# Convolution steps of a DeltaNet layer, moved one by one between VectorE's other work

## The reference

```python
h = jnp.einsum('btd,dc->btc', x, w_in)
qa, ka, va, za, ba, aa, qb, kb, vb, zb = jnp.split(h, offsets, axis=-1)
ya = _deltanet_group(qa, ka, va, za, ba, aa, conv_w, a_log, dt_bias, norm_w)
yb = _swa_group(qb, kb, vb, zb, sinks)
y = jnp.einsum('btc,cd->btd', jnp.concatenate([ya, yb], axis=-1), w_out)
return _layernorm(DEEPNORM_ALPHA * x + y, ln_g, ln_b)
```

```python
v_new = u_c - jnp.einsum('bhcd,bhde->bhce', w_c, s)
o = jnp.einsum('bhcd,bhde->bhce', q_c, s) + jnp.einsum('bhcs,bhse->bhce', qk_c, v_new)
s = s * gt[..., None, None] + jnp.einsum('bhcd,bhce->bhde', k_c, v_new)
```

## Time and profile before

| | |
|---|---|
| runs (3), median | 1091.87 us |
| lowest to highest | 1090.0 to 1093.45 us |
| profiled execution, its own time | 1090.27 us |
| its span, first to last instruction | 1088.5 us |
| TensorE busy | 1064.2 us, 98% |
| VectorE busy | 688.7 us, 63% |
| ScalarE busy | 532.7 us, 49% |
| GpSimd busy | 115.9 us, 11% |
| granted TensorE clock, mean | 0.999 of full speed |

### The profile page before, as it was taken

How to read it: one execution, slowest core, us unless ns; L and a number is a source line. 1 busy time by engine, 2 the same in 40 slices (tenths; PEclk the granted TensorE clock), 3 DMA queues, 4 the chain that set the end, 5 groups by cost and what they waited for, 6 DMA issues and landing times.

```text
span 1088.5 us, 19513 instructions
## 1 busy us (share of the span) xinstructions
PE 1064.2 (98%) x7212; PEld 846.5 (78%) x7212; DVE 688.7 (63%) x2081; ACT 532.7 (49%) x1557; POOL 115.9 (11%) x152
## 2 busy tenths in 40 slices
PE   7999999999999999999999999999999999999997
PEld 5877787778778787777887878787787878787885
DVE  5285959584665747576365665757537575758565
ACT  4557675754636454363354535435344555564300
POOL 3413132134100000020000000002000000002210
PEclk9999999999999999999999999999999999999999
DMA  8967475665553626253562551715454343622432
GB/s 282 315 209 262 163 274 195 243 208 183 201 205 109 237 73 235 87 185 98 175 228 93 165 215 46 265 49 185 132 179 157 126 157 128 215 73 63 137 116 77
DMA packets 58430, 183.55 MB, mean 169 GB/s; under 512 B 8480, under 2 KB 21216, under 8 KB 45024
## 3 DMA queue, kind: packets, MB, share of 16 engines
q1 hardware_dynamic: 58192, 182.05, 48.7%
q10 hardware_dynamic: 144, 0.26, 0.1%
HBM read 138.22 MB, written 44.07 MB: 167 GB/s over the span
## 4 chain that ended last, share of the span: by engine, by line
PE 65%; DVE 6%; DMA 2%; issue 1%; ACT 0%; SPq 0%; DVEq 0%
PE bank L849 33%; PE bank L900 10%; PE bank L1137 4%; PE bank L957 2%; PE bank L990 2%; PE bank L972 2%; PE bank L1107 1%; PE bank L1120 1%; PE bank L1117 1%; PE bank L1121 1%; DVE y_cols L1797 1%; DVE y_step L1793 1%; PE bank L1030 1%; PE bank L1045 1%; PE bank L1115 1%
## 5 line engine op out<-in xcount | busy, mean ns | idle before, releaser
L849 PE MATMUL bank<-xr,w 128*128 128x512 f32 x2496 | 653.9, 405 | 7.4 <-DVE xr L1534 7.4
L849 PEld LDWEIGHTS bank<-xr,w 128*128 128x128 f32 x2496 | 449.8, 189 | 101.7 <-issue 9.8
L900 PE MATMUL bank<-wo,y_split 128*128 128x512 f32 x432 | 114.4, 404 | 0.0
L900 PEld LDWEIGHTS bank<-wo,y_split 128*128 128x128 f32 x432 | 77.0, 189 | 14.6 <-issue 0.7
L1582 DVE SCALAR_TENSOR_TENSOR kq<-conv_in,convw_all,kq 128x512 f32<-128x512 f32 x96 | 77.3, 806 | 7.8 <-ACT conv_in L1191 5.8
L1487 ACT ACTIVATE o_scaled<-bank 128x128 f32<-128x128 f32 x64 | 17.7, 277 | 124.5 <-PE bank L1121 124.3
L1353 ACT ACTIVATE score<-score,neg_max 128x256 f32<-128x256 f32 (+1 forms) x128 | 62.7, 493 | 29.0 <-DVE neg_max L1759 29.0
L1919 DVE TENSOR_SCALAR steps<-bank,nb_rk 128x128 f32<-128x128 f32 x64 | 22.3, 348 | 63.9 <-PE bank L1117 63.9
L1922 DVE SCALAR_TENSOR_TENSOR state<-state,cols_all,bank 128x128 f32<-128x128 f32 x64 | 22.2, 347 | 63.2 <-PE bank L1120 63.2
L1793 DVE TENSOR_TENSOR y_step<-blocks,y_cols 128x60 f32<-128x60 f32 (+14 forms) x240 | 50.3, 210 | 12.1 <-DMA blocks<-n_spill 3.3
L783 POOL TENSOR_TENSOR xr<-y_tile,xr 128x256 fp32r<-128x256 f32 x8 | 6.0, 774 | 455.1 <-ACT xr L1172 455.1
(11 more groups left out here) (217 smaller groups left out, 1628.3 us busy)
## 6 DMA issues: line engine op xcount, KB each, us to landing
w<-w_split SPq DMA_DIRECT2D x78, 1024.0 KB, 5.4
w_split<-w SPq DMA_DIRECT2D x26, 1024.0 KB, 5.1
blocks<-n_spill SPq DMA_DIRECT2D x32, 256.0 KB
y_spill<-y_out SPq DMA_DIRECT2D x30, 256.0 KB, 5.8
x_tile<-w_in SPq DMA_DIRECT2D x13, 512.0 KB, 6.1
y_tile<-w_in SPq DMA_DIRECT2D x12, 512.0 KB, 6.4
y_tile<-y_spill SPq DMA_DIRECT2D x12, 512.0 KB, 6.1
x_tile<-x SPq DMA_DIRECT2D x12, 512.0 KB, 3.9
```

The lines of the kernel that those rows point to most:

```text
L849: ins = nc.tensor.matmul(bank[JOBS[at].bank][:], w[:, turn % 3, wp, k, :], xr[:, xp, k], start=(step == 0), stop=(step == 3 * KT - 1))
L900: ins = nc.tensor.matmul(bank[JOBS[at].bank][:], y_place(t)[:, yp, k], wo[:, k, wp, half * UNIT:(half + 1) * UNIT], start=(step == 0), sto ...
```

## The change

`conv(m, c, step)` now does one step, and a head is nine parts of one step in place of six. For slots 0 to 2 the calls of `convs` stay where they were. From slot 3 on:

- no convolutions are taken ahead of the base inverse (the call at place 0.2); the call of at most one part behind the first gate stays;
- behind the second division `convs` takes as many parts as bring the head to three, which is the whole of `q`;
- a new `conv_gap` takes at most one part ahead of VectorE's wait for `tr` and one ahead of its wait for `kv`, in each chunk; with one more behind `state` in chunks 0 and 1 this makes the other six: `k` in chunk 0, `v` in chunk 1. In slots 7 and 11, where the raw `v` comes later, `v` goes to chunk 2;
- `slopes(n + 1)` moves from behind the second division to behind `state` of chunk 2.

```diff
--- before.py
+++ after.py
@@ -1568,21 +1568,20 @@
 
             slopes(0)
 
-            def conv(m, c, half):
+            def conv(m, c, step):
 
                 own = kq[:, m % 2]
                 acc = (own[:, 1], own[:, 0], v_ch[:])[c]
                 i = m % AH
-                if half == 0:
+                if step == 0:
                     after(dve, raw_copied, m, c + 1)
                     after(dve, tail_put, m, 1)
-                for step in (0,) if half == 0 else (1, 2):
-                    if step > 0:
-                        after(dve, conv_step, m, 2 * c + step)
-                    ins = nc.vector.scalar_tensor_tensor(acc, conv_in[:, c, step:step + UNIT],
-                                                         convw_all[:, i, c, step:step + 1], acc, ALU.mult, ALU.add)
-                    ins.then_inc(conv_step.sem if step < CONV - 2 else conv_ready.sem, 1)
-                if c == 2 and half == 1:
+                else:
+                    after(dve, conv_step, m, 2 * c + step)
+                ins = nc.vector.scalar_tensor_tensor(acc, conv_in[:, c, step:step + UNIT],
+                                                     convw_all[:, i, c, step:step + 1], acc, ALU.mult, ALU.add)
+                ins.then_inc(conv_step.sem if step < CONV - 2 else conv_ready.sem, 1)
+                if c == 2 and step == CONV - 2:
                     nc.vector.tensor_copy(tails[:, i], conv_in[:, :, UNIT:]).then_inc(tail_saved.sem, 1)
                     if m < SLOTS - 1:
                         after(dve, tail_saved, m, 1)
@@ -1697,16 +1696,21 @@
             beta_place = [0]
             conv_place = [0]
 
-            def convs(n, f, most=6):
-
-                while conv_place[0] < 6 * SLOTS and most > 0:
-                    m, part = divmod(conv_place[0], 6)
-                    c, half = divmod(part, 2)
+            def convs(n, f, most=9):
+
+                while conv_place[0] < 9 * SLOTS and most > 0:
+                    m, part = divmod(conv_place[0], 9)
+                    c, step = divmod(part, 3)
                     if JOBS[JOB_AT["qkv"[c], m]].end > n + f + 1e-6:
                         return
-                    conv(m, c, half)
+                    conv(m, c, step)
                     conv_place[0] += 1
                     most -= 1
+
+            def conv_gap(n, f):
+
+                if n >= AH - 1:
+                    convs(n, f, 1)
 
             def split_y(e):
 
@@ -1865,7 +1869,8 @@
                     x_low(s + 1, 1)
                 if n < AH:
                     weight_rest(n - 1, "bq")
-                convs(n, 0.2)
+                if n < AH - 1:
+                    convs(n, 0.2)
                 after_jobs(n, at.base)
                 if n == SLOTS - 1:
                     split_y(9)
@@ -1896,14 +1901,14 @@
                 after(dve, inv_done, n, 4)
                 nc.vector.transpose(t32[QUAD:HALF, :, 0:QUAD], quad_tiles(bank[5])[0:QUAD]).then_inc(t_ready.sem, 1)
                 divide(n, 1)
-                if n < SLOTS - 1:
+                if n < AH - 1:
                     slopes(n + 1)
                 if i == AH - 1 and s < SBS - 1:
                     after_jobs(n, JOBS[JOB_AT["bT", s + 1]].end - n)
                 if n == SLOTS - 1:
                     split_y(10)
                     split_y(11)
-                convs(n, at.p32)
+                convs(n, at.p32, 9 if n < AH - 1 else max(0, 9 * (n + 1) + 3 - conv_place[0]))
                 after_jobs(n, at.step0)
                 for c in range(CH):
                     one = slice(c, c + 1)
@@ -1915,17 +1920,26 @@
                     nc.vector.scalar_tensor_tensor(resid, bank[4][:, 0:P], col(EG)[:, one], v_tok[:, c], ALU.mult, ALU.subtract)\
                         .then_inc(resid_ready.sem, 1)
                     after_jobs(n, at.chunk(c, 1 / 3))
+                    conv_gap(n, at.p64 if c == 0 else at.chunk(c - 1))
                     after(dve, tr_done, n, c + 1)
                     nc.vector.tensor_scalar(v_new, bank[6][:, 0:P], nb_rk[:, one], None, ALU.mult).then_inc(v_new_ready.sem, 1)
                     after_jobs(n, at.chunk(c, 2 / 3))
+                    conv_gap(n, at.p64 if c == 0 else at.chunk(c - 1))
                     after(dve, kv_done, n, c + 1)
                     nc.vector.scalar_tensor_tensor(state[:, i], state[:, i], col(EGT)[:, one], bank[4][:, P:2 * P],
                                                    ALU.mult, ALU.add).then_inc(state_ready.sem, 1)
                     if n == SLOTS - 1 and c < 3:
                         split_y(12 + c)
                     after_jobs(n, at.chunk(c, 0.8))
-                    if c < 3:
-                        convs(n, (at.p64, at.chunk(0), 1)[c], 1 if n == AH - 1 and c < 2 else 6)
+                    if n < AH - 1:
+                        if c < 3:
+                            convs(n, (at.p64, at.chunk(0), 1)[c])
+                    elif c < 2:
+                        convs(n, (at.p64, at.chunk(0))[c], 1)
+                    elif c == 2:
+                        convs(n, 1)
+                        if n < SLOTS - 1:
+                            slopes(n + 1)
                     if c == CH - 1:
                         if t is not None and i == AH - 2:
                             split_y(t + 1)
```

## The result

The changed kernel takes 1095.42 us, the median of 12 runs (1092.68 to 1096.88); the kernel before, 12 runs on the same chip, takes 1091.11 us (1088.78 to 1095.61). The ratio is 1.0032, with a 95% interval from 1.0019 to 1.0045: 3.5 us slower by the ratio, 2.1 to 4.9 by its interval (the two medians lie 4.3 apart). The forecast was 1095.7 us, 3.9 us or 0.35% above the kernel before, in a range from 1091.3 to 1099. Sign and size came out. One term of the sum was too big, though, one was too small, and one was missing, as the experiments show.

A forecast was written before the change was run, and what follows sets the result against it. TensorE, busy 1064.2 of 1088.5 us, was taken as the bound, VectorE costing time only where TensorE waits for it. -0.64 + 4.5 gave +3.9 us on the median of 1091.87: 1095.7 us, range 1091.3 to 1099.

The forecast's parts named there:

- (1): Convolution steps everywhere: each takes 752 ns at the median, their count stays 144, and no DMA is moved past another.
- (5): Chunk 1 of slots 4, 5, 6, 8, 9, 10: a step behind the added half delays v_new; cost 4.5 us.
- (2): Ahead of the base inverse, slots 4-6, 8-10, 12-14: three q steps leave; gain 0, as slot 12 waits for a DMA.
- (3): Behind the second division: less work ahead of chunk 0, felt by TensorE in slots 6 and 10 alone; gain 0.64 us.
- (4): Gaps of chunks 0 and 1: six steps, one ahead of each VectorE wait for TensorE, hidden where free; cost 0.
- (6): Behind chunk 1's delayed v_new: state, the moved bias products and ScalarE's SiLU make nothing more late; no cost.
- B: Rival: TensorE's later waits for state and the inverse shrink, giving 1.7 us back; +2.2 us, 1094.1 us; chance 0.25.
- C: Rival: chunk 1's step is free and lighter VectorE ends TensorE's waits for it; -4.7 us, 1087.1 us; chance 0.07.
- D: Rival: steps in the gaps take up to 1.25 us each; +8.3 us, 1100 us; chance 0.13.

The follow-up runs named there:

- the first experiment: Changed kernel with chunk 1's convolution step moved ahead of the added output half, before v_new: 1090.63 us, ratio 0.9984 to the kernel before.
- experiment 2: Changed kernel with two convolution steps in place of one behind the added half at the six places: 1099.44 us, ratio 1.0070 to the kernel before.
- experiment 5: Kernel before plus one spare VectorE instruction of a step's shape behind the added half at the six places: 1095.35 us, ratio 1.0030.
- experiment 3: Changed kernel with the three q steps taken ahead of the base inverse again: 1094.95 us, ratio 1.0032 to the kernel before.
- experiment 4: Changed kernel with blocks loaded ahead of the weight tile in slot 12: one run, 1091.26 us against 1090.36 for the kernel before.
- experiment 6: Changed kernel with two steps again ahead of the inverse's third transpose in slots 0 to 2: one run, 1095.77 us against 1091.64 for the kernel before.
- experiment 8: Changed kernel with chunk 1's step before the half, earlier blocks, q steps rearranged in slots 0 to 2, statistics behind v_new: 1086.10 us, ratio 0.9957 to the kernel before.
- the ninth experiment: Kernel of experiment 8 with one step in place of two ahead of the inverse's third transpose in slots 0 to 2: 1086.23 us, ratio 0.9953 to the kernel before.

## Why the prediction was nearly right

**Parts (1) and (5): the mechanism and the six places, right; the price, too high.** The step that sank the change was found in the order of the code and in the earlier trace rows: TensorE at `kv` waited for `v_new` without slack, so what is put ahead of `v_new` is paid in full. Experiments 1, 2 and 5 show it by taking it out, doubling it and doing it alone. The term 6 x 0.75 = 4.5 us was 6 x 0.65 = 3.9. I took the recorded duration; what counts is from start to start, and VectorE starts the next instruction before the record of this one ends. The earlier trace rows showed that already: the statistics start at 325.52, are recorded at 0.69 us, and `v_new` starts at 326.13, 0.61 us later. Held against the kernel before's own profile the six cost 3.6 us, because slot 8 had by chance a wait of its own there, which the first experiment's kernel, at 1.78 us from `tr` to `kv`, does not have; in the changed kernel slot 8 takes 2.44 us from `tr` to `kv` like slot 5, where the prediction had more, and slot 6 takes 2.58, where it had 2.7.

The Trainium skill, "Perfetto Trace Analysis", section on optimizing Scalar and DVE operations, says that the profiled latency has about twice the fixed overhead that keeps the engine busy, some 60 ns on SBUF, because the half that acknowledges the write overlaps with the next instruction. By that the price of a step would be some 0.06 us below its record, an estimate. The trace agrees nearly: 0.08 us overlap here, and none where the next step waits for the result. By the Trainium skill, "VectorE: DVE Perf Modes", section on the TRN2 errata, which the prediction set against the row, the six would cost 3.6 us as an estimate; the 0.65 measured lies between its 0.594 and the 0.75 of the row.

**Part (2): right.** The inverse of slot 12 waits for a DMA with or without the steps (experiments 3 and 4); VectorE waits 4.6 us for it in the changed kernel, the number forecast, and TensorE's wait stayed, 1.1 us where it was 1.0.

**Part (3): right, a little too small.** In chunk 0 of slot 6 TensorE now goes from L1115 to L1117 as forecast, in 0.22 us in place of 0.54. But the wait also stretched the way from there to L1120. First L1120 of the kernel before, then the three of the changed kernel:

```profile
446.52 0.38 PE L1120 MATMUL bank<-steps,k_dec 128*128 128x128 f32 x2
```

```profile
446.77 0.38 PE L1115 MATMUL bank<-state,kq 128*128 128x128 f32 x2
...
446.99 0.39 PE L1117 MATMUL bank<-steps,y_inv 128*128 128x128 f32 x2
...
448.61 0.38 PE L1120 MATMUL bank<-steps,k_dec 128*128 128x128 f32 x2
```

From L1115 to L1120 it is 1.84 us in place of 2.25 (444.27 to 446.52), 0.41 less, and about the same in slot 10: 0.8 us in all, where the prediction's term is 0.64.

**Part (4): right.** In slot 12, the tightest, the steps lie in the gaps and VectorE still idles ahead of `v_new`, 0.36 us where 0.27 was worked out; slots 12 and 13 kept their 53.0 and 51.4 us:

```profile
855.39 0.35 DVE L1925 TENSOR_SCALAR steps<-bank,nb_rk 128x128 f32<-128x128 f32 x1 [0.36 <-PE bank L1117]
855.66 0.74 DVE L1581 SCALAR_TENSOR_TENSOR kq<-conv_in,convw_all,kq 128x512 f32<-128x512 f32 x1
...
855.88 0.40 PE L1120 MATMUL bank<-steps,k_dec 128*128 128x128 f32 x2
```

Slot 14 is 1.4 us longer, 1.1 of it the wait for a weight tile that comes and goes; slot 3 is 0.6 us longer, as in all experiments, the one built on the kernel before among them.

**Part (6): right.** No wait for `state`, for SiLU or for the moved bias products was added.

**Missed:** part (1) counted the steps and left it there; that a part is now one step and not two changes each call that is limited by a count, and one such call in slots 0 to 2 gave 0.96 us, of which some 0.4 stayed (experiment 6).

So the sum has three errors, and all point the same way: 0.6 us too much for the steps, 0.2 too little for part (3), and a gain of about 0.4 left out. Corrected it is 3.9 - 0.8 - 0.4 = +2.7 us, inside the measured 2.1 to 4.9; without the six steps' 3.9 it is -1.2 us, 0.9989, inside the first experiment's interval around 0.9984. That the forecast's +3.9 lies nearer to the ratio's +3.5 than the corrected sum does is luck: the 0.8 us between +2.7 and +3.5 are within the spread of the measurement, and I have no term for them.

**The rivals.** B: the waits that were to shorten did not (0.5 us for `state`; in slots 7 and 11, 2.2 less 1.1 for the inverse, 1.1 where 1.3 was before). C: the point from which it decides was the right one, but its gain does not come from the lighter stretches; the first experiment makes the step free, and its ratio is 0.9984 with 1 inside the interval, where C had 0.9957. D: from slot 4 on the steps in the gaps and at the six places ran at the median; behind 260 us no step of the changed kernel is recorded above 0.8 us.

## What to carry to other kernels

When work is cut fine to fill an in-order engine's gaps, ask of each gap whether the filler stands ahead of or behind the instruction that waits; ahead it lies in idle time, behind it delays the one that the bound engine needs. An engine with 37% idle time can have none at such a place, and a list of waits may hide it: compare the bound engine's start-to-start times between places with the same work between. When the unit of a list changes, look again at each call that takes a fixed number of units.

## What the runs showed of the hardware

- A step of 128 by 512 on VectorE, recorded at 0.73 us, cost 0.65 us ahead of an instruction that does not depend on it (experiment 5), and 0.78 ahead of one that does (experiment 2).
- The list of TensorE's waits, as read from the trace, leaves short ones out and can give others too small. It shows none at the place of the earlier trace rows where `kv` came 0.16 us late, and in slots 1 and 2 of the kernel before it gives 0.15 us for a wait that cost 0.32 from start to start.
- Behind a matmul that was waited for, TensorE lost some 0.1 us more: from `kv` to the next `ks` 1.94 us in place of 1.83 (experiment 8).
- Removing a wait on the bound engine paid in full at the six places, less than half in slots 0 to 2 of the changed kernel (0.4 of 0.96 us), where a DMA for ScalarE was waited for next, and not at all in the ninth experiment, where VectorE's next result was late by more than was won.
